# Second phase of a two-phase mixer kernel: the order of the small rounds inside a body changes

## The chip, the cores and the metric

The kernel runs on one core of a Trainium2 chip. The metric is device time in microseconds for one launch. Three runs of the kernel before gave 2612.58, 2613.08 and 2613.16 us; the median is 2613.08 us. One further execution was profiled.

## The reference, cut to what matters

One layer reads a prompt of 4096 tokens and 8 running streams of 16 tokens, all of width 1024. After an RMS norm, one projection feeds two groups of heads: a gated linear attention (4 heads) and an RWKV-7 group (8 heads of 64). The second group is the one that the change touches:

```
xm = p_shift + rwkv_mu * (prev - p_shift)          # token shift
r, kr, vr, wd, ad = jnp.split(xm, ...)             # 512, 512, 512, 64, 64 columns
w = jnp.exp(-DECAY * jax.nn.sigmoid(w0 + jnp.tanh(wd) @ w_up))   # low rank, width 64
a = jax.nn.sigmoid(a0 + ad @ a_up)                 # low rank, width 64
kk = kr * k_k;  kr = kr * (1 + (a - 1) * k_a)
kk = kk / max(sqrt(sum over head of kk*kk), 1e-12) # a sum over each head of 64
S_t = S_{t-1} (diag(w_t) - kk_t^T (a_t*kk_t)) + v_t^T k_t ;  y_t = S_t r_t
y = group_norm(y) * ln_w + ln_b + bonus;  o = y * silu(z_r)
```

Both groups' outputs go through one output projection, a second RMS norm and the residual.

## The kernel before

The program has two phases that follow each other. The first (to about 1004 us) is the gated linear attention group, and is not touched. The second is the RWKV group, cut into 17 blocks of tokens: block 0 holds the 8 streams (128 tokens), blocks 1 to 16 hold 256 tokens of the prompt each. A block is worked off in chunks of 64 tokens, four in a block (two in block 0). The chunks are a chain: the state S after one chunk is needed by the next.

TensorE's work (PE below) falls in two sorts. The filler is the projection of a block from `r_hT`, in six rounds of 48 matmuls (named x4, x6 for the keys, x0, x2 for r, x8, x10 for v, each 2 of 13 column groups) and one of 24 (x12, the low-rank inputs wd and ad); the hi and lo halves of the numbers make three products. A round is issued in thirds of 8 matmuls, called pieces (`piece`, L1616). Small rounds hang on it: `lwa0` and `lwa2` (L1643, the low-rank products for w and a), `kn0` and `kn2` (L1671, the head sums of the squared keys), `xs0` and `xs1` (L1660, the blocks of the triangular matrix), `bs0` and `bs2` (L1671, the head sums for the bonus), `centre` and `variance` (L1817 and L1822, the group norm).

The chain of a chunk is: `meet` (L1765 and L1749, reads S), `scores` of the next chunk (L1695), `unknowns` (L1779), `turn` of the next chunk (L1706, L1709), `solve` (L1719, L1726), `advance` (L1790, new state, and L1803, y), `join` (L1736). `join` waits for `keep_w`, a copy on VectorE (DVE below) of PE's L1726 result from bank B to `r_Wt` (L2208). `next` on DVE (L2243, L2245) makes the new S, for which the next `meet` waits.

The order of all of it is written out by hand in four tables, one an engine: `PE_BODY`, `ACT_BODY`, `DVE_BODY`, `POOL_BODY`, and one for the DMA queue of SyncE (SP), which stays. A table is the order in one body; body e works the chain of block e's four chunks, projects block e + 2, and, for the names with a minus, finishes block e + 1 (`xs`, `bs`, and on GpSimd, POOL below, `kappa`, `r` and `invert`). Numbers behind a colon are the chunk in the body. `out` marks a point at which the jobs of the output projection may be put; in the last two bodies the pieces that have no block left are replaced by pieces of that projection (`room`), which begins at the token x2 of the last body but one. Each engine takes its list strictly in order, and waits on semaphores. There are four PSUM banks for rounds; a round waits until the one four before it has been read.

ScalarE (ACT) does the table functions: `tanh_w` (L1888), `tanh` (L1901, which makes the inputs of `decay`), `squares` (L1911), `gamma` (L1931 to L1937), `rnorm` (L1919, L1921), `deviation` (L1983, L1985), and copies out of PSUM (`taken`, `odd`, `turned`, `z1`, `keep_y`, `join_e`). DVE does `decay` (L2106 and four scans L2109), `clamp` (L2117), `k_factor` (L2133), `unit` (L2126), `k_prime` (L2140, L2141), `even` (L2235, without which `advance` can't start), `beta` (L2157), `a` (L2162), `rkk` (L2149), `mixed` (L2093), `normed` (L2265, four L2268), `gated` (L2275, L2278), `low` (L2282) and `masked` (L2195). POOL inverts the triangular blocks in 60 dependent steps (L1557, L1559), between a store and a load through scratch DRAM on each side; `turn_inverse` on DVE (L2203) then transposes the result, and `solve` of the next block's first chunk, in the last quarter of the body, waits for it.

Of the kernel before, what the change touches and what calls it, by code (L numbers as in the profile page):

```python
# [59 lines left out]
def tiles(b):  # L60

    return 1 if b == 0 else BLK // P
# [58 lines left out]
def nchunks(b):  # L121
    return 2 if b == 0 else 4


def first_chunk(b):
    return CHUNKS.index((b, 0))


def last_chunk(b):
    return first_chunk(b) + nchunks(b) - 1  # L130
# [126 lines left out]
def gla_phase(nc, t, c):  # L257
# [719 lines left out]


PE_BODY = """
    meet:0 scores:1 x12*3 -xs0 -xs1 unknowns:0 turn:1 x4 out x4*3 solve:1 advance:0 join:1 x4*2 -bs0 -bs2 meet:1  # L980
    out scores:2 centre:0 x6*3 unknowns:1 turn:2 x6*2 out x6 variance:0 lwa0 solve:2 advance:1 join:2 x0*4 out
    meet:2 scores:3 x0*2 lwa2 x2 unknowns:2 turn:3 x2*2 out x2*2 solve:3 advance:2 join:3 x2 kn0 kn2 x8 meet:3
    out scores:4 x8*5 unknowns:3 turn:4 centre:1 x10 out x10*2 solve:4 advance:3 join:4 x10*3 variance:1 out
""".split()
ACT_BODY = """
    -deviation:1 taken:x12 -high:1 odd:0 tanh_w out turned:1 z1:1 keep_y:0 join_e:1 taken:x4 out centred:0
    squares:0 odd:1 turned:2 out taken:x6 deviation:0 z1:2 keep_y:1 join_e:2 tanh:lw0 tanh:la0 out squares:2
    high:0 taken:x0 tanh:lw2 tanh:la2 odd:2 turned:3 out gamma keep_y:2 z1:3 join_e:3 taken:x2 rnorm:0 out
    rnorm:2 taken:x8 odd:3 turned:4 centred:1 out z1:4 keep_y:3 join_e:4 taken:x10 load_h out
""".split()  # L990
DVE_BODY = """
    -mixed:x10 -normed:1 masked:1 zc:0 -gated:1 mixed:x12 even:0 -strict:0 out -strict:1 -low:1 keep_w:1 next:0
    join_o:1 -bonus:0 mixed:x4 out zc:1 -bonus:2 masked:2 even:1 out mixed:x6 keep_w:2 normed:0 next:1 join_o:2
    gated:0 out zc:2 low:0 masked:3 mixed:x0 decay out even:2 keep_w:3 next:2 join_o:3 clamp:0 mixed:x2 clamp:2
    out zc:3 k_factor masked:4 unit:0 unit:2 k_prime even:3 mixed:x8 out beta a keep_w:4 next:3 join_o:4 rkk out
""".split()
POOL_BODY = "-kappa -r -invert".split()
SP_BODY = """
# [166 lines left out]
def rwkv_phase(nc, t, c):  # L1165
# [13 lines left out]
    with ExitStack() as ctx:  # L1179
        def sb(name, shape, dt=F32):  # L1180
            return ctx.enter_context(nc.sbuf_tensor("r_" + name, shape, dt))
# [6 lines left out]
        def sig(name, n, size, step=1):  # L1188
            s = Count(ctx.enter_context(nc.semaphore("r_" + name)), name, n, size, step)
            signals.append(s)  # L1190
            return s
# [3 lines left out]
        centre = sb("centre", [P, P])  # L1195
# [77 lines left out]
        def par_s(name, g):  # L1273
            return sc[:, SC[name] + g:SC[name] + g + 1]
# [4 lines left out]
        def plane(b, p):  # L1279
            return ops[:, b % 3, p, :, 0:tiles(b) * P]  # L1280
# [25 lines left out]
        ss_out = sig("ss_out", 8, 1, 16)  # L1306
# [41 lines left out]
        y_full = sig("y_full", 1, NQ)  # L1348
# [504 lines left out]
        def _(act):  # L1853
# [8 lines left out]
            def pair_of(b, r):  # L1862
                n = tiles(b) * P
                act.wait_ge(d_full.sem, d_full.at(ROUND_NO[b, r], 1))
                return bank_of((b, r))[:, 0:2 * n].rearrange("p (g t) -> p g t", g=2)
# [24 lines left out]
            def tanh(arg):  # L1890
                b, r = arg
                n = tiles(b) * P
                pair = pair_of(b, r)
                g0 = int(r[2])
                if r == "lw0" and b:
                    act.wait_ge(op_ok.sem, op_ok.at(b - 1, 2))
                    act.wait_ge(kap_ok.sem, kap_ok.at(b - 1, 2))
                s, bias = (lw_ok, "w0h") if r[1] == "w" else (la_ok, "a0h")
                out = gin[:, :, 0:n] if r[1] == "w" else plane(b, T_)
                for g in range(2):  # L1900
                    act.activation(out[:, g0 + g, :], pair[:, g, :], ACT.Tanh, scale=0.5,  # L1901
                                   bias=par_s(bias, g0 + g)).then_inc(*s.up(b))
# [106 lines left out]
            def out_rstd(tile):  # L2009
# [6 lines left out]
                act.activation(s[:, 3:4], s[:, 2:3], ACT.Exp, scale=-0.5, bias=const(K_LNM)).then_inc(*os_ok.up(tile))  # L2016

            does = {"taken": taken, "tanh_w": tanh_w, "tanh": tanh, "squares": squares, "rnorm": rnorm,
                    "gamma": gamma, "load_h": lambda b: load_h(b + 2), "centred": centred, "deviation": deviation,
                    "high": high_part, "ow_high": split_out, "o_squares": out_squares, "o_rstd": out_rstd,  # L2020
# [376 lines left out]
```

## Time and profile before

| what | value |
|---|---|
| median of three runs | 2613.08 us |
| profiled execution, its own time | 2613.44 us |
| its span | 2611.7 us |
| PE busy | 2480.8 us, 95% |
| ACT, DVE, POOL busy | 51%, 50%, 24% |
| PE clock granted, mean | 0.975 of full |

The span is the time from the first to the last instruction; what lies around it is 1.74 us. Busy is the union of an engine's instructions. PE's matmuls overlap in the array, so that one has a duration of some 270 ns where the next one starts after 109 ns; PE's stalls are read from starts and from the view of waits, not from its busy share. A body has 70.1 us in the middle of the phase.

### The profile page before, as it was taken

The numbers are of one execution on the slowest core, as the hardware profiler recorded it, in microseconds if no ns is written. First come the engines' busy times: TensorE is split into PE (matmuls) and PEld (weight loads), VectorE is DVE, ScalarE is ACT, GpSimd is POOL, SyncE is SP. The second block draws the span as 40 slices with busy tenths as digits, with TensorE's granted clock in tenths as the row PEclk, the third lists the DMA queues.
The fourth block names the chain that finished last, engine by engine and source line by source line (L and its number), as shares of the span: only waits on it lengthen the run. The fifth ranks groups of instructions, "written<-read, shape, count | busy, mean of one in ns | idle before, by whom it ended". The sixth has DMA issues, their size and how long they took to land.

```text
span 2611.7 us, 70434 instructions
## 1 busy us (share of the span) xinstructions
PE 2480.8 (95%) x30628; PEld 1891.0 (72%) x30628; DVE 1295.8 (50%) x2646; ACT 1330.2 (51%) x2368; POOL 623.7 (24%) x1104
## 2 busy tenths in 40 slices
PE   4899999999999995979999999999999997899998
PEld 4677777777777775768888888888888885544443
DVE  4333344433333324456667666776776765442222
ACT  6345566556555544335555555555555553343332
POOL 0000000000000001245555555555555554100000
PEclk9799999999999997989999999999999997999999
DMA  4112222122111112102122212222122214245444
GB/s 188 57 56 76 75 71 66 62 74 89 60 58 53 41 41 76 47 16 72 59 67 67 67 55 67 67 67 59 49 64 56 61 51 146 82 143 159 152 145 137
DMA packets 171027, 202.47 MB, mean 78 GB/s; under 512 B 90080, under 2 KB 125216, under 8 KB 166368
## 3 DMA queue, kind: packets, MB, share of 16 engines
q1 hardware_dynamic: 166352, 180.66, 22.2%
q10 hardware_dynamic: 4368, 17.30, 1.9%
q8 instruction: 243, 3.98, 0.6%
q14 instruction: 64, 0.52, 0.1%
HBM read 117.65 MB, written 80.28 MB: 76 GB/s over the span
## 4 chain that ended last, share of the span: by engine, by line
PE 47%; DVE 4%; POOL 4%; ACT 2%; DMA 2%; issue 1%; SPq 1%; DVEq 0%; POOLq 0%
PE r_d L1616 30%; POOL r_inv L1559 2%; POOL r_inv_tmp L1557 2%; PE r_d L1671 2%; PE r_RZ L1790 2%; PE r_A L1695 1%; PE r_RZ L1765 1%; PE r_A L1719 1%; PE r_d L1643 1%; PE r_d L1660 1%; PE r_RZ L1779 1%; PE r_RY L1803 1%; PE r_d L1817 1%; PE r_RY L1749 1%; PE r_B L1736 1%
## 5 line engine op out<-in xcount | busy, mean ns | idle before, releaser
L1616 PE MATMUL r_d<-r_hT,w_hi 128*128 128x256 f16 (+1 forms) x3536 | 583.4, 272 | 15.2 <-DMA r_hT<-scratch_hT 15.2
L567 PE MATMUL d<-hT,w_hi 128*128 128x256 f16 (+1 forms) x3264 | 525.9, 270 | 1.4 <-DVE hT L840 1.4
L1616 PE MATMUL r_d<-r_hT,w_lo 128*128 128x256 f16 (+1 forms) x1768 | 475.6, 272 | 0.0
L567 PE MATMUL d<-hT,w_lo 128*128 128x256 f16 (+1 forms) x1632 | 436.6, 270 | 0.0
L1616 PEld LDWEIGHTS r_d<-r_hT,w_hi 128*128 128x128 f16 x3536 | 336.7, 99 | 82.4 <-issue 24.3
L567 PEld LDWEIGHTS d<-hT,w_hi 128*128 128x128 f16 x3264 | 315.6, 98 | 51.1 <-issue 12.5
L1557 POOL TENSOR_TENSOR r_inv_tmp<-r_inv 64x30 f32<-64x30 f32 (+14 forms) x480 | 251.6, 524 | 290.5 <-DMA r_inv<-scratch_blocks 254.1
L1616 PE MATMUL r_d<-w_hi,r_ops 128*128 128x512 f16 x1056 | 317.4, 381 | 2.1 <-DVE w_lo L2286 1.7
L1559 POOL TENSOR_TENSOR r_inv<-r_inv,r_inv_tmp 64x30 f32<-64x30 f32 (+14 forms) x480 | 268.9, 560 | 37.6
L1506 POOL MEMSET r_run_s<- 128x128 f16 x1 | 0.2, 205 | 1000.9 <-POOLq L266 1000.9
L1882 ACT ACTIVATE r_praw<-r_d,r_sc 128x256 f32<-128x256 f32 (+1 forms) x221 | 92.5, 467 | 240.9 <-PE r_d L1616 240.8
L1616 PE MATMUL r_d<-w_lo,r_ops 128*128 128x512 f16 x528 | 201.0, 381 | 0.0
L1616 PEld LDWEIGHTS r_d<-w_hi,r_ops 128*128 128x128 f16 x1056 | 103.1, 98 | 129.1 <-issue 7.7
L1616 PEld LDWEIGHTS r_d<-r_hT,w_lo 128*128 128x128 f16 x1768 | 174.3, 99 | 25.6 <-issue 5.2
L567 PEld LDWEIGHTS d<-hT,w_lo 128*128 128x128 f16 x1632 | 160.4, 98 | 17.4
L567 PE MATMUL d<-w_hi,hT 128*128 128x512 f16 x528 | 157.0, 379 | 0.0
L2093 DVE SCALAR_TENSOR_TENSOR r_ops<-r_d,r_sc,r_praw 128x256 f32<-128x256 f32 (+1 forms) x204 | 87.8, 472 | 109.4 <-ACT r_praw L1882 106.9
L2006 ACT ACTIVATE r_xb<-r_d 128x512 f32<-128x512 f32 x66 | 39.5, 598 | 194.1 <-PE r_d L1616 194.1
L2297 DVE TENSOR_TENSOR r_ops<-r_d,w_hi 128x512 f32<-128x512 f32 x66 | 45.6, 691 | 183.0 <-ACT r_xb L2006 182.9
L558 PE MATMUL tr<-diag,x_tok 128*128 128x128 f32 x528 | 74.0, 285 | 36.5 <-DVE diag L832 36.5
L1567 POOL TENSOR_TENSOR r_ops<-r_ops,r_gin 128x1024 f32<-128x1024 f32 (+1 forms) x17 | 38.9, 2290 | 264.5 <-DVE r_scr L2149 264.5
L567 PE MATMUL d<-w_lo,hT 128*128 128x512 f16 x264 | 100.1, 379 | 0.0
(270 smaller groups left out, 4737.6 us busy)
## 6 DMA issues: line engine op xcount, KB each, us to landing
x_tok<-in_x SPq DMA_DIRECT2D x33, 512.0 KB, 4.3
r_ops<-in_x SPq DMA_DIRECT2D x33, 512.0 KB, 4.2
out_y<-r_ops SPq DMA_DIRECT2D x33, 512.0 KB, 2.9
scratch_hT<-hT SPq DMA_DIRECT2D x16, 1024.0 KB, 6.8
r_hT<-scratch_hT ACTq DMA_DIRECT2D x16, 1024.0 KB, 4.8
scratch_mg<-m_hl SPq DMA_DIRECT2D x33, 256.0 KB, 2.0
r_zr<-scratch_zr SPq DMA_DIRECT2D x33, 256.0 KB, 3.3
r_bon<-scratch_bonus SPq DMA_DIRECT2D x33, 256.0 KB, 3.9
```

The costliest lines, as they stand in the source:

```text
L558: mm = pe.matmul(tr_bank[half][:, k * P:(k + 1) * P], x_tok[:, tile % 2, (4 * half + k) * P:(4 * half + k + 1) * P], diag[:, tile % 2, :], ...
L567: mm = pe.matmul(out, lhs(k, a, w), rhs(k, a, w), start=(n == 0), stop=(n == len(terms) - 1))
L1557: step(pool.tensor_tensor(tmp, inv[0:n, 0:u, u:u + 1].to_broadcast([n, u, w]), inv[0:n, u:u + 1, u + 1:32].to_broadcast([n, u, w]), ALU.mult))
L1559: step(pool.tensor_tensor(inv[0:n, 0:u, u + 1:32], inv[0:n, 0:u, u + 1:32], tmp, ALU.add))
L1567: pool.tensor_tensor(plane(b, K_), plane(b, K_), gin[:, :, 0:n], ALU.mult).then_inc(*kap_ok.up(b))
L1616: mm = pe.matmul(out, lhs(k, a, w), rhs(k, a, w), start=(m == 0), stop=(m == 3 * KT - 1))
L1671: mm = pe.matmul(out[:, g * n:(g + 1) * n], headsum[:, :], scr[:, g0 + g, 0:n], start=True, stop=True)
L1790: mm = pe.matmul(half(RZ, 0)[hrows(h), g, :], bu[:, s, h, 0, g, :], uv(h, g), start=True, stop=True)
L1882: ins = act.activation(out[:, g], src[:, g], ACT.Identity, scale=par_s("mu", g0 + g))
L2006: act.activation(o_junk[h], bank_of(("out", tile, h))[:, :], ACT.Square, accum_out=st[:, tile % 2, h:h + 1]).then_inc(*os_ok.up(tile))
L2093: dve.scalar_tensor_tensor(out=out[:, g], in0=pair[:, g], scalar=par_s("mu1", g0 + g), in1=before[:, g], op0=ALU.mult, op1=ALU.add).then_i ...
L2297: dve.tensor_tensor(t_c[:, h * 512:(h + 1) * 512], bank_of(("out", tile, h))[:, :], npost[:, h * 512:(h + 1) * 512], ALU.mult).then_inc(*o ...
```

## The change

The tables are written in another order. On PE, `lwa0` moves from the second chunk of a body to the end of the first, `lwa2` from the third to the second, `kn0` and `kn2` from the end of the third to the end of the second, ahead of most of x0, so that x0, x2, x8, x10 (r and v) come after all that hangs on the keys. `xs1` goes behind `unknowns:0` and `turn:1`, `bs2` behind the next `scores`, `centre:0` and `variance:0` each half a chunk to a chunk later. ACT and DVE follow: `decay`, the clamps, `k_factor`, `unit`, `k_prime`, `beta`, `a`, `rkk`, and `normed:0`, `gated:0`, `low:0` change places. The opening (blocks 0 and 1 before the first chunk) is made from the same tables and changes too. In `tanh` one wait is new: `la0` writes into a plane that an older block's chunks still read. Of the tables the diff shows PE's and DVE's second and third lines.

```diff
 PE_BODY = """
...
-    out scores:2 centre:0 x6*3 unknowns:1 turn:2 x6*2 out x6 variance:0 lwa0 solve:2 advance:1 join:2 x0*4 out
-    meet:2 scores:3 x0*2 lwa2 x2 unknowns:2 turn:3 x2*2 out x2*2 solve:3 advance:2 join:3 x2 kn0 kn2 x8 meet:3
+    meet:1 scores:2 -bs2 x6*3 unknowns:1 turn:2 x6*2 out x6 lwa2 solve:2 advance:1 join:2 centre:0 kn0 kn2 x0*2
+    out meet:2 scores:3 x0*4 unknowns:2 turn:3 variance:0 x2 out x2*2 solve:3 advance:2 join:3 x2*3 x8 meet:3
...
 DVE_BODY = """
...
-    gated:0 out zc:2 low:0 masked:3 mixed:x0 decay out even:2 keep_w:3 next:2 join_o:3 clamp:0 mixed:x2 clamp:2
+    clamp:0 out clamp:2 k_factor masked:3 zc:2 unit:0 unit:2 k_prime out even:2 beta normed:0 keep_w:3 gated:0
...
                 if r == "lw0" and b:
                     act.wait_ge(op_ok.sem, op_ok.at(b - 1, 2))
                     act.wait_ge(kap_ok.sem, kap_ok.at(b - 1, 2))
+                if r == "la0" and b >= 3:
+                    act.wait_ge(y_full.sem, y_full.at(last_chunk(b - 3), 1))
+                    if b == 3:
+                        act.wait_ge(ss_out.sem, ss_out.at(0, 8))
```

Lines of ACT's and DVE's code lie 5 further down in the changed kernel (L2208 is L2213), those of PE's one (L1736 is L1737). Below, DVE in the third chunk of a body. Before, these rows stand between the reading of x0 and the copy for `join:3`:

```order
L2106 TENSOR_SCALAR r_gin<-r_gin 128x1024
L2109 SCALAR_TENSOR_TENSOR r_gin<-r_run_p,r_gin 128x256 x4
L2235 COPY r_bu<-r_RZ 64x256
L2208 COPY r_Wt<-r_B 128x128
L2243 TENSOR_TENSOR r_S<-r_RZ,r_S 128x256
L2245 TENSOR_TENSOR r_S<-r_S,r_gL 128x256
L2213 COPY r_TT<-r_B 32x4x32
```

In the changed kernel, from `unit` to `next:2` in the same chunk:

```order
L2131 SCALAR_TENSOR_TENSOR r_ops<-r_ops,r_sc 128x256 x4
L2145 TENSOR_TENSOR r_ops<-r_ops,r_scr 128x1024
L2146 SCALAR_TENSOR_TENSOR r_ops<-r_ops 128x1024
L2240 COPY r_bu<-r_RZ 64x256
L2162 SCALAR_TENSOR_TENSOR r_ops<-r_ops,r_gin 128x1024
L2270 TENSOR_TENSOR r_yT<-r_yT,r_d 128x512
L2273 TENSOR_SCALAR r_yT<-r_yT,r_sc,r_lnb_s 128x128 x4
L2213 COPY r_Wt<-r_B 128x128
L2280 TENSOR_TENSOR r_yT<-r_yT,r_bon 128x512
L2283 TENSOR_TENSOR r_yT<-r_yT,r_zr 128x512
L2248 TENSOR_TENSOR r_S<-r_RZ,r_S 128x256
```

The copy to `r_Wt` stood right behind the copy to `r_bu` (`even:2`); now `beta` and `normed:0`, six instructions, stand between them, and `unit` and `k_prime`, another six, ahead of `even:2`.

DVE at the end of the second chunk, between the copy for `join:2` and the new state. Before (`normed:0` between them):

```order
L2208 COPY r_Wt<-r_B 128x128
L2265 TENSOR_TENSOR r_yT<-r_yT,r_d 128x512
L2268 TENSOR_SCALAR r_yT<-r_yT,r_sc,r_lnb_s 128x128 x4
L2243 TENSOR_TENSOR r_S<-r_RZ,r_S 128x256
L2245 TENSOR_TENSOR r_S<-r_S,r_gL 128x256
```

In the changed kernel `decay` stands there:

```order
L2213 COPY r_Wt<-r_B 128x128
L2111 TENSOR_SCALAR r_gin<-r_gin 128x1024
L2114 SCALAR_TENSOR_TENSOR r_gin<-r_run_p,r_gin 128x256 x4
L2248 TENSOR_TENSOR r_S<-r_RZ,r_S 128x256
L2250 TENSOR_TENSOR r_S<-r_S,r_gL 128x256
```

The new state of the second chunk now comes behind the scans instead of behind the group norm's scaling.

PE at the end of the second chunk of a body. Before, from `variance:0` to `join:2`:

```order
L1822 MATMUL r_d<-r_y_sq,r_headmean 128x512
L1643 MATMUL r_d<-r_lor,r_up 128x256 x4
L1719 MATMUL r_A<-r_bu,r_sxq 64x64 x8
L1726 MATMUL r_B<-r_TD,r_sxq 32x32 x8
L1790 MATMUL r_RZ<-r_bu 64x64 x8
L1803 MATMUL r_RY<-r_sxq,r_bu 64x64 x8
L1736 MATMUL r_B<-r_TT,r_Wt 32x32 x8
```

In the changed kernel, from `lwa2` to `kn2`:

```order
L1644 MATMUL r_d<-r_lor,r_up 128x256 x4
L1720 MATMUL r_A<-r_bu,r_sxq 64x64 x8
L1727 MATMUL r_B<-r_TD,r_sxq 32x32 x8
L1791 MATMUL r_RZ<-r_bu 64x64 x8
L1804 MATMUL r_RY<-r_sxq,r_bu 64x64 x8
L1737 MATMUL r_B<-r_TT,r_Wt 32x32 x8
L1818 MATMUL r_d<-r_yT,r_centre 128x512
L1672 MATMUL r_d<-r_scr,r_headsum 128x256 x4
```

The low-rank products here were the first pair and are now the second, and the head sums of the keys follow the chain directly.

## Rows read from the trace of the kernel before

**Rows 1.** Stretches: length; busy PE, PEld, DVE, ACT, POOL; PE clock; DMA share; GB/s

```profile
1004.00:1180.00 176.00, 142.12 (x1966) 123.58 (x1968) 84.15 (x212) 63.72 (x126) 61.61 (x134) 0.86 0.20 54
1180.00:2162.00 982.00, 980.09 (x17466) 819.99 (x17461) 681.40 (x1434) 559.77 (x1033) 520.21 (x882) 1.00 0.21 61
...
1460.31:1530.41 70.10, 70.07 (x1251) 58.59 (x1252) 48.94 (x103) 40.21 (x75) 37.38 (x64) 1.00 0.22 62
```

**Rows 2.** PE's waits from 1180 to 2162 us (total, times, longest)

```profile
PE r_B L1726 <- DVE r_TD L2203: 1.5, 3, 0.8
```

**Rows 3.** The chain of waits in that body (start us, us, what)

```profile
1460.31 0.61 PE r_RZ L1765 x16
...
1462.27 2.73 PE r_d L1616 x24
1464.99 2.01 PE r_d L1660 x64
...
1468.34 3.60 PE r_d L1616 x32
1471.94 0.61 PE r_A L1719 x16
...
1474.01 0.37 PE r_B L1736 x16
...
1476.23 1.73 PE r_d L1671 x8
...
1487.80 0.86 PE r_d L1822 x2
1488.65 1.06 PE r_d L1643 x8
```

**Rows 4.** The same body, ACT in order of time (start us, us, instruction)

```profile
1506.24 1.06 ACT L1931 ACTIVATE r_gam<-r_gin 128x1024 f32<-128x1024 f32 x1 [0.72 <-DVE r_gin L2109]
...
1511.00 1.28 ACT L1916 ACT_TABLE_LOAD   x1
...
1515.65 0.72 ACT L1921 ACTIVATE r_ops<-r_ops,consts 128x512 f32<-128x512 f32 x1
```

**Rows 5.** The same body, DVE in order of time

```profile
1463.68 1.12 DVE L2268 TENSOR_SCALAR r_yT<-r_yT,r_sc,r_lnb_s 128x128 f32<-128x128 f32 x4
...
1492.02 2.32 DVE L2268 TENSOR_SCALAR r_yT<-r_yT,r_sc,r_lnb_s 128x128 f32<-128x128 f32 x4
...
1502.38 3.83 DVE L2109 TENSOR_TENSOR_SCAN r_gin<-r_run_p,r_gin 128x256 f32<-128x256 f16 x4
...
1518.24 1.23 DVE L2140 TENSOR_TENSOR r_ops<-r_ops,r_scr 128x1024 f32<-128x1024 f32 x1
...
1520.52 0.41 DVE L2235 COPY r_bu<-r_RZ 64x256 f32<-64x256 f32 x1
...
1521.90 1.22 DVE L2157 SCALAR_TENSOR_TENSOR r_ops<-r_ops,r_gin 128x1024 f32<-128x1024 f32 x1
...
1524.17 0.70 DVE L2203 STREAM_TRANSPOSE r_TD<-r_TT 128x512 f32<-128x512 f32 x1
```

**Rows 6.** The same body, POOL's last step of the inversion

```profile
1516.28 0.35 POOL L1561 TENSOR_SCALAR r_inv<-r_inv 64x32 f32<-64x32 f32 x1
```

**Rows 7.** Two stalls of PE, and the stretch behind each (columns of rows 1)

```profile
2233.00:2237.00 4.00, 0.79 (x33) 0.61 (x27) 0.71 (x1) 0.39 (x1) 0.00 (x0) 1.00 0.43 68
2237.00:2241.00 4.00, 4.00 (x58) 2.90 (x54) 1.59 (x5) 1.79 (x3) 0.00 (x0) 0.57 0.01 4
...
2166.00:2169.00 3.00, 0.76 (x22) 0.62 (x20) 3.00 (x8) 0.00 (x0) 0.00 (x0) 0.96 0.55 218
2169.00:2179.00 10.00, 7.02 (x142) 6.38 (x139) 6.74 (x12) 5.14 (x9) 0.00 (x0) 0.50 0.21 40
```

**Rows 8.** PE's waits, whole program (total, times, longest)

```profile
PE r_A L1706 <- DVE r_sxq L2195: 4.3, 2, 3.6
PE r_d L1660 <- DVE r_ops L2162: 4.3, 1, 4.3
```

More of the change, by code:

```diff
@@ L979 @@
 PE_BODY = """
-    meet:0 scores:1 x12*3 -xs0 -xs1 unknowns:0 turn:1 x4 out x4*3 solve:1 advance:0 join:1 x4*2 -bs0 -bs2 meet:1
-    out scores:2 centre:0 x6*3 unknowns:1 turn:2 x6*2 out x6 variance:0 lwa0 solve:2 advance:1 join:2 x0*4 out
-    meet:2 scores:3 x0*2 lwa2 x2 unknowns:2 turn:3 x2*2 out x2*2 solve:3 advance:2 join:3 x2 kn0 kn2 x8 meet:3
-    out scores:4 x8*5 unknowns:3 turn:4 centre:1 x10 out x10*2 solve:4 advance:3 join:4 x10*3 variance:1 out
+    meet:0 scores:1 x12*3 -xs0 unknowns:0 turn:1 -xs1 x4 out x4*3 solve:1 advance:0 join:1 x4*2 lwa0 -bs0 out
@@ L984 @@
+    meet:1 scores:2 -bs2 x6*3 unknowns:1 turn:2 x6*2 out x6 lwa2 solve:2 advance:1 join:2 centre:0 kn0 kn2 x0*2
+    out meet:2 scores:3 x0*4 unknowns:2 turn:3 variance:0 x2 out x2*2 solve:3 advance:2 join:3 x2*3 x8 meet:3
+    out scores:4 x8*5 unknowns:3 turn:4 centre:1 out x10*3 solve:4 advance:3 join:4 x10*3 variance:1 out
 """.split()
 ACT_BODY = """
-    -deviation:1 taken:x12 -high:1 odd:0 tanh_w out turned:1 z1:1 keep_y:0 join_e:1 taken:x4 out centred:0
-    squares:0 odd:1 turned:2 out taken:x6 deviation:0 z1:2 keep_y:1 join_e:2 tanh:lw0 tanh:la0 out squares:2
@@ L988 @@
-    high:0 taken:x0 tanh:lw2 tanh:la2 odd:2 turned:3 out gamma keep_y:2 z1:3 join_e:3 taken:x2 rnorm:0 out
-    rnorm:2 taken:x8 odd:3 turned:4 centred:1 out z1:4 keep_y:3 join_e:4 taken:x10 load_h out
+    -deviation:1 taken:x12 odd:0 tanh_w turned:1 out -high:1 z1:1 keep_y:0 join_e:1 taken:x4 tanh:lw0 out
+    tanh:la0 odd:1 turned:2 squares:0 out taken:x6 tanh:lw2 tanh:la2 z1:2 keep_y:1 squares:2 join_e:2 centred:0
+    gamma out rnorm:0 rnorm:2 taken:x0 odd:2 turned:3 out deviation:0 z1:3 join_e:3 high:0 keep_y:2 taken:x2 out
@@ L990 @@
+    taken:x8 odd:3 turned:4 out centred:1 z1:4 keep_y:3 join_e:4 taken:x10 load_h out
 """.split()
 DVE_BODY = """
-    -mixed:x10 -normed:1 masked:1 zc:0 -gated:1 mixed:x12 even:0 -strict:0 out -strict:1 -low:1 keep_w:1 next:0
-    join_o:1 -bonus:0 mixed:x4 out zc:1 -bonus:2 masked:2 even:1 out mixed:x6 keep_w:2 normed:0 next:1 join_o:2
-    gated:0 out zc:2 low:0 masked:3 mixed:x0 decay out even:2 keep_w:3 next:2 join_o:3 clamp:0 mixed:x2 clamp:2
-    out zc:3 k_factor masked:4 unit:0 unit:2 k_prime even:3 mixed:x8 out beta a keep_w:4 next:3 join_o:4 rkk out
+    -mixed:x10 zc:0 masked:1 -normed:1 mixed:x12 even:0 -gated:1 -strict:0 out -strict:1 -low:1 keep_w:1 next:0
@@ L996 @@
+    join_o:1 mixed:x4 out -bonus:0 zc:1 masked:2 -bonus:2 even:1 out mixed:x6 keep_w:2 decay next:1 join_o:2
+    clamp:0 out clamp:2 k_factor masked:3 zc:2 unit:0 unit:2 k_prime out even:2 beta normed:0 keep_w:3 gated:0
+    next:2 low:0 join_o:3 mixed:x0 out mixed:x2 masked:4 zc:3 a rkk even:3 mixed:x8 out keep_w:4 next:3 join_o:4
+    out
 """.split()
```

## The prediction, made before the changed kernel ran

> **What bounds the kernel now.** I read the table of busy time by stretches first. The changed phase has three parts [rows 1]: an opening of 176 us in which PE is busy 142 us at 0.86 of its clock, a middle of 982 us with PE busy 980 us at full clock, and an end with stalls. The reader is to see that the middle has nothing to give: the view of PE's waits has 1.5 us in those 982 us, all of them on the transposed inverse [rows 2], and the body of 70.10 us is a train of PE work. The change neither adds nor removes PE work, so the middle can only lose, or stay; gains can come from the opening and the end alone. Next I read one body of the middle in the chain of waits, for PE's durations, and in order of time for ACT and DVE. All places below are counted from the body's first `meet`, +0 being 1460.31 us [rows 3].
>
> **PE's new timetable.** Pieces from [rows 3]: `meet` with `scores` 1.96 (1460.31 to 1462.27), three projection pieces 2.73, both `xs` 2.01, `unknowns` with `turn` about 1.4 (1467.00 to 1468.34), four pieces 3.60, `solve` to `join` 2.07 and `join` itself 0.37, two `kn` or `bs` 1.73, `variance` or `centre` 0.9, a low-rank pair 1.06. In the changed order these add up, without a stall, to 17.8 for the second chunk's `meet`, 35.5 for the third's, and in the third chunk: scores done +37.5, four pieces of x0 +41.1, `unknowns` and `turn` +42.5, `variance` +43.4, three pieces of x2 +46.1, `advance` about +47.1, `join:3` +48.2. The body's sum is as before.
>
> **Who must be there at +48.2.** `join:3` waits for the copy to `r_Wt`, and DVE takes its list in order. I follow the chain back to its start. The second chunk's L1726 is done at +29.6; DVE copies it (done +29.95) and then runs `decay`: 0.7 for the addition and 3.83 for the scans [rows 5], done +34.4. ACT's `gamma` waits for that. Before, it goes from 1506.24 [rows 4], and its two activations of 1.06 and the small copy are 2.3: done +36.9. Then two `rnorm`, 5.37 together (1511.00 to 1516.37, [rows 4], table loads in it): done +42.3. DVE has the clamps, `k_factor` and the masks done by +40 and waits for that. From +42.3: the second `unit` 0.9, `k_prime` 2.28 (1518.24 to 1520.52, [rows 5]), `even:2` 0.34, `beta` 1.14 (1521.90, next instruction behind it), one multiplication of `normed` 0.7, four scalings, copy 0.3. `even:2` comes at +45.9, in time for `advance` at +47.1. The four scalings take 1.12 where POOL is idle (1463.68) and 2.32 in the inversion (1492.02) [rows 5]; the inversion ends at +56.3 [rows 6], so here they are slow. Sum: 42.3 + 0.9 + 2.3 + 0.3 + 1.2 + 0.7 + 2.3 + 0.3 = +50.3 at the least; `join:3` has been waiting since +48.2. Before, the copy for this `join` stood right behind `even:2`, and `join` never waited.
>
> I take 3.0 us a body for this stall. The lower end is 2.1 (sum above). Upper end: `k_prime` and `beta` run in the inversion now, which no row of before shows; if they are slowed as the scalings are in absolute terms, 0.3 us an instruction (2.32 less 1.12, over four), three of them give 0.9; I allow as much again for what differs between bodies, which makes 4.0. 3.0 is the lower end with the 0.9 that the rows bear out.
>
> The Trainium skill bears on this ("SBUF — State Buffer", section "SBUF: two separate sides"): a DVE instruction in a two-port mode or with two SBUF inputs and a GpSimd instruction exclude each other for a whole instruction. The slow scalings agree [rows 5]. By that rule `k_prime` and `beta` wait too, the sum is at the upper end and not the lower, and the inversion loses what they take.
>
> **The clock.** A stall of that length on PE is followed by half clock in the places where the trace has one. Behind the stall in which PE is busy 0.79 of 4 us, the next 4 us have 0.57 with PE busy all through; behind the one with 0.76 of 3 us, 10 us have 0.50 [rows 7]. Full speed is 2.4 GHz, the half 1.2. Where PE is busy with projections, 4 us at 0.57 cost 0.43 x 4 = 1.7 us. Behind `join:3` stand four pieces of projection, dense work, so I take the short kind, and 1.5 us a body. Bounds: 0 (the clock stays), and 5 (10 us at 0.50, all filled).
>
> The Trainium skill ("TensorE: Matmul & The Clock Gate", "What's actually happening") says that the throttled state is the default and activity releases it. By that a drop in every body would be no surprise, and dense work behind it ends it soon.
>
> **What else moves, and costs nothing in a body.** The inversion: `xs1` is 1.4 us later on PE, but DVE's `strict:0` and `strict:1` stood behind `even:0` anyway, which comes 1 us earlier since `unknowns` goes ahead of `xs1`; with `gated:1` ahead of them they end at about +9.3, before at +9.5. SP's queue keeps its order. If POOL's 60 steps get longer by 1 to 3 us, `turn_inverse` has that room, since `solve:4` is itself 3 to 5 us later by the stall, and DVE is freed: before, it reached that point at +63.9 (1524.17) [rows 5] straight from `a`. The one new wait, `la0` for y of an older block, stands behind `keep_y:0`, which has waited for the same; behind it on ACT `odd:1` is queued, 5 us away. `decay` between `join:2`'s copy and the second chunk's new state: S is ready at 34.4 + 0.9 = +35.3 against `meet` at +35.5; hidden by 0.2, and if the cover fails the price is about 0.5 a body. `kn2` wants `squares:2`, at +32.0 against +32.8. Tanh's table load is saved once a body, on an engine that has room.
>
> **Opening and end.** In the opening `kn0` and `kn2` come before x0, so ACT's and DVE's chain for block 0 starts two rounds earlier, and the wait of 4.3 us of `xs0` for `a` [rows 8] shrinks to about 1; each block pays 1.5 us of PE waiting for `squares:2`. The first `turn`'s wait of 3.6 for the mask [rows 8] falls to about 1.5, with the half clock behind it. The third chunk of block 0 has `beta` ahead of its state steps. Together I take -3, bounds -8 and +2. In the last body but one `strict:1` stands behind jobs of the output weights that wait for ACT; ACT's `turned:1` now goes ahead of its half of them, and the last inversion starts some 2 us earlier. `normed:0` ahead of the copy costs about 2 in the same body. I take 0, bounds -4 and +4.
>
> **The sum.** The bodies of blocks 1 to 14 have all of it, a block two ahead whose `k_prime` stands in the third chunk and a tile to normalise: 14 bodies. 14 x (3.0 + 1.5) = 63; opening -3; end 0; the 1.5 us of [rows 2] go: +58.5. Against the profiled execution's own 2613.44 that is 2672; the median of the runs, 2613.08, lies 0.36 below it. I forecast 2671 us.
>
> **Rivals.** (1) The stall, but the clock stays full. For: the trace has only a few stalls to go by, all where the work around them is thinner than in the middle. Against: the one in 3 us of [rows 7] is no longer than the new one, and was followed by it. 14 x 3.0 - 4.5 = +37.5: 2650. (2) Faster, because the wait at `join:3` isn't there. It decides at one point: whether DVE is through with the scalings before +48.2, which it would be if `rnorm` ended 2.1 us earlier than I have it. For: all of it hangs on sums of a dozen durations, and the opening then gives its 3 to 5. Against: `gamma`, the two `rnorm` and the DVE work behind them have no slack to lose, and each has its row. 2613 - 5: 2608. (3) No stall at `join:3`, but POOL is slowed by `unit`, `k_prime` and `beta` inside the inversion by more than the 1.5 us that the inverse has, for which PE has waited three times already [rows 2]: 14 x 1 - 4 = +10: 2623. (4) The stall with the long kind of half clock each time: 14 x (3.0 + 4.5) - 4.5 = +100: 2714.
>
> **How the numbers follow.** Forecast 0.52, (1) 0.24, (2) 0.12, (3) 0.05, (4) 0.07. The range should leave 2 in 10: (2) and half of (4) and (3) are out. The forecast's own ends are 14 x 2.1 + 14 x 0.8 - 8 = +33 and 14 x (4.0 + 2) + 4 = +88; with (1), and its lower end 14 x 2.1 - 6 = +23, the range is 2632 to 2706. A difference of 0.2%, 5 us, is about what can be told from none: faster by more 0.09, within it 0.05, slower by more 0.86.
>
> **What would show it.** In the changed profile, PE's waits from 1180 us on have a line L1737 <- DVE r_Wt L2213 with 14 or 15 times and 30 to 55 us, where before there is 1.5 us in all; in the same body DVE goes without a gap from the second L2131 through L2145, L2146, L2240, L2162, L2270 and L2273 to L2213; each body is 73 to 76 us long; PE's clock in the middle stretch falls below 1.00, to about 0.95; the wait on the inverse is gone there. In the opening the wait L1661 <- L2167 is 1 us in place of 4.3. Wrong would be: a body of 70.1 us, or a stall at another wait (`meet` for S, L1672 for the squares), or a stall of 3 us with the clock at 1.00.

## The result, and the profile after

The changed kernel takes 2684.8 us (median of four runs, 2680.1 to 2687.3) where the kernel before takes 2612.8: ratio 1.0274, 95% interval 1.0256 to 1.0292. It is 72 us slower. The forecast was 2671, the range 2632 to 2706.

The table of busy time by stretches of the changed kernel comes first: the opening and the middle of [rows 1], and one body, which now has 75.05 us (columns as in [rows 1]).

```profile
1004.00:1180.00 176.00, 143.40 (x1970) 122.73 (x1972) 91.76 (x213) 63.55 (x127) 67.37 (x134) 0.87 0.20 55
1180.00:2162.00 982.00, 939.32 (x16279) 776.31 (x16276) 695.99 (x1335) 500.43 (x949) 521.82 (x819) 0.97 0.20 57
1330.99:1406.04 75.05, 71.93 (x1250) 59.52 (x1249) 53.69 (x103) 38.55 (x74) 40.02 (x63) 0.98 0.21 58
```

The opening has hardly changed. In the middle PE is busy for 939 of 982 us instead of 980, and its clock is 0.97 instead of 1.00. A body has the same instructions as before, and DVE is busy in it for 53.7 us instead of 48.9: the same work on DVE has become longer. PE's waits in the middle (total, times, longest), against [rows 2]:

```profile
PE r_B L1737 <- DVE r_Wt L2213: 39.5, 13, 3.2
PE r_RZ L1766 <- DVE r_S L2250: 1.1, 4, 0.4
```

One line has taken the place of the wait for the inverse: `join:3` waits for the copy to `r_Wt`, 3.0 us each time. In the 14 bodies of blocks 1 to 14 (1179.5 to 2235.2 us) it is 42.5 us in 14 times, over the whole program 50.1 us in 18 times; the wait of `xs0` in [rows 8] has gone from 4.3 to 1.0, and a wait of the head sums for the squares is new:

```profile
PE r_B L1737 <- DVE r_Wt L2213: 50.1, 18, 5.1
...
PE r_d L1672 <- ACT r_scr L1916: 4.2, 3, 1.5
...
PE r_d L1661 <- DVE r_ops L2167: 1.0, 1, 1.0
```

The stall and what follows it, by stretches (columns as before):

```profile
1376.50:1379.50 3.00, 2.93 (x72) 2.46 (x71) 3.00 (x4) 2.04 (x4) 2.84 (x3) 1.00 0.00 0
1379.50:1383.00 3.50, 0.45 (x22) 0.31 (x18) 3.46 (x8) 0.00 (x0) 3.09 (x6) 1.00 0.02 5
1383.00:1387.00 4.00, 4.00 (x38) 3.02 (x31) 3.83 (x8) 1.28 (x3) 3.47 (x7) 0.62 0.25 65
```

PE is busy 0.45 of 3.5 us, DVE all through; then PE has four microseconds of dense products at 0.62 of its clock. The granted clock costs 1.7 us in twelve of the 14 bodies and 3.4 in the other two (the first and the thirteenth, of 76.1 and 76.9 us), 27.3 us together. The chain of waits has the same place from PE's side: the four projection pieces behind `join:3` take 5.27 us, where four had 3.60 in [rows 3].

```profile
1383.24 5.27 PE r_d L1617 x32
```

And DVE in order of time, from the copy for `join:2` to the copy for `join:3` (start us, us, instruction, and in brackets the idle time ahead of it):

```profile
1360.87 0.29 DVE L2213 COPY r_Wt<-r_B 128x128 f32<-128x128 f32 x1 [0.16 <-PE r_B L1727]
...
1361.79 3.96 DVE L2114 TENSOR_TENSOR_SCAN r_gin<-r_run_p,r_gin 128x256 f32<-128x256 f16 x4
...
1368.08 2.65 DVE L2138 TENSOR_SCALAR r_scr<-r_ops,r_sc 128x256 f32<-128x256 f32 x4
...
1372.18 2.99 DVE L2131 SCALAR_TENSOR_TENSOR r_ops<-r_ops,r_sc 128x256 f32<-128x256 f32 x4
1375.28 1.40 DVE L2145 TENSOR_TENSOR r_ops<-r_ops,r_scr 128x1024 f32<-128x1024 f32 x1
1376.60 1.61 DVE L2146 SCALAR_TENSOR_TENSOR r_ops<-r_ops 128x1024 f32<-128x1024 f32 x1
...
1380.32 2.22 DVE L2273 TENSOR_SCALAR r_yT<-r_yT,r_sc,r_lnb_s 128x128 f32<-128x128 f32 x4
1382.46 0.28 DVE L2213 COPY r_Wt<-r_B 128x128 f32<-128x128 f32 x1
```

No instruction from the second on, those left out included, has idle time in brackets: the list lasts from 1360.87 to 1382.46, 21.6 us. PE needs 18.7 us from the end of `solve:2` to the point at which it wants `join:3`. That was not in the prediction, which counted from ACT's `rnorm`. In the trace the last step of `rnorm` ends at 1373.44, and DVE, behind its own list, comes to the half of `unit` that reads it at 1373.60, so the two chains meet there within 0.2 us; the experiments take them apart.

```profile
1372.72 0.72 ACT L1926 ACTIVATE r_ops<-r_ops,consts 128x512 f32<-128x512 f32 x1
```

### The profile page after: what moved, and what is told of

It reads as the page before. It is cut to its first block, busy times and chain, and to the rows that moved or that the text cites. A ratio compares the mean times of both kernels' runs of the same rounds, so it can differ in the third digit from the quotient of the medians.

```text
span 2685.6 us, 70433 instructions
## 1 busy us (share of the span) xinstructions
PE 2508.6 (93%) x30628; PEld 1900.6 (71%) x30628; DVE 1368.2 (51%) x2646; ACT 1305.9 (49%) x2354; POOL 667.4 (25%) x1104
## 4 chain that ended last, share of the span: by engine, by line
PE 44%; DVE 13%; issue 2%; POOL 1%; DMA 1%; ACT 1%; SPq 0%; DVEq 0%; POOLq 0%; ACTq 0%
PE r_d L1617 30%; DVE r_gin L2114 2%; DVE r_ops L2131 2%; PE r_A L1696 1%; PE r_d L1672 1%; DVE r_scr L2138 1%; PE r_d L1644 1%; PE r_RZ L1766 1%; PE r_d L1661 1%; DVE r_yT L2273 1%; PE r_RZ L1791 1%; PE r_A L1720 1%; DVE r_ops L2146 1%; PE r_RZ L1780 1%; DVE r_sxq L2200 1%
## 5 line engine op out<-in xcount | busy, mean ns | idle before, releaser
L1617 PE MATMUL r_d<-r_hT,w_hi 128*128 128x256 f16 (+1 forms) x3536 | 607.4, 279 | 14.9 <-DMA r_hT<-scratch_hT 14.3
L1617 PE MATMUL r_d<-r_hT,w_lo 128*128 128x256 f16 (+1 forms) x1768 | 487.7, 278 | 0.0
L1617 PEld LDWEIGHTS r_d<-r_hT,w_hi 128*128 128x128 f16 x3536 | 346.8, 101 | 89.5 <-issue 21.3
L1558 POOL TENSOR_TENSOR r_inv_tmp<-r_inv 64x30 f32<-64x30 f32 (+14 forms) x480 | 277.9, 579 | 447.0 <-DMA r_inv<-scratch_blocks 410.6
L567 PEld LDWEIGHTS d<-hT,w_hi 128*128 128x128 f16 x3264 | 315.6, 98 | 51.4 <-issue 12.6
L1560 POOL TENSOR_TENSOR r_inv<-r_inv,r_inv_tmp 64x30 f32<-64x30 f32 (+14 forms) x480 | 285.3, 594 | 37.6
L1617 PEld LDWEIGHTS r_d<-w_lo,r_ops 128*128 128x128 f16 x528 | 52.0, 99 | 63.2 <-issue 2.1
```

The costliest lines, as they stand in the source:

```text
L567: mm = pe.matmul(out, lhs(k, a, w), rhs(k, a, w), start=(n == 0), stop=(n == len(terms) - 1))
L1558: step(pool.tensor_tensor(tmp, inv[0:n, 0:u, u:u + 1].to_broadcast([n, u, w]), inv[0:n, u:u + 1, u + 1:32].to_broadcast([n, u, w]), ALU.mult))
L1560: step(pool.tensor_tensor(inv[0:n, 0:u, u + 1:32], inv[0:n, 0:u, u + 1:32], tmp, ALU.add))
L1617: mm = pe.matmul(out, lhs(k, a, w), rhs(k, a, w), start=(m == 0), stop=(m == 3 * KT - 1))
```

## The experiments

The kernel before ran beside each group of kernels; its medians there were 2612.7, 2614.1, 2612.2 and 2612.3 us, and ratios are against those.

**The keys behind the join.**

```diff
-    ... zc:2 unit:0 unit:2 k_prime out even:2 beta normed:0 keep_w:3 gated:0
-    next:2 low:0 join_o:3 mixed:x0 out ...
+    ... zc:2 unit:0 out even:2 normed:0 keep_w:3 gated:0
+    next:2 low:0 join_o:3 unit:2 k_prime beta mixed:x0 out ...
```

> The changed kernel with the third chunk's list on DVE in another order: the second unit, k_prime and beta stand behind join_o:3, so that only even:2 and normed stand ahead of the copy for join:3. My theory is that the whole loss is DVE's queue ahead of that copy: by my timetable normed, which waits for the variance at +43.4 and ACT's two steps behind it, is then done at about +48.2 and the copy at +48.5, against join:3 at +48.7, so the stall of 3.1 us and the half clock behind it both go, the body is 70.1 to 70.6 us again, and the time is 2684.8 - 14 x 5 = about 2615 (2608 to 2625). Rival A, the half clock comes from the new order on PE (thinner work round the head sums) and not from the stall: only 14 x 3.1 goes, 2641. Rival B, POOL's inversion, slowed by k_prime and beta beside it, becomes late and PE waits for the transposed inverse instead: 1 us a body or more, 2630.

Measured: 2701.3 us, ratio 1.034 (1.0324 to 1.0355). The time lies outside every branch: it is slower than the changed kernel. Of the mechanisms, rival B's did come, and larger than its number: PE waits for the inverse. PE's waits from 1180 to 2200 us:

```profile
PE r_B L1727 <- DVE r_TD L2208: 26.2, 13, 2.1
PE r_B L1737 <- DVE r_Wt L2213: 21.9, 13, 1.9
PE r_RZ L1780 <- DVE r_Zc L2226: 13.4, 9, 1.7
```

The wait at `join:3` fell from 3.0 to 1.7 us and two others came up. For the first, DVE and ACT in order of time show the reason:

```profile
1379.63 0.69 DVE L2270 TENSOR_TENSOR r_yT<-r_yT,r_d 128x512 f32<-128x512 f32 x1 [4.27 <-ACT r_d L1990]
```
```profile
1372.10 1.28 ACT L1921 ACT_TABLE_LOAD   x1
...
1377.03 1.28 ACT L1986 ACT_TABLE_LOAD   x1
...
1379.02 0.58 ACT L1990 ACTIVATE r_d<-r_d 128x512 f32<-128x512 f32 x1
```

DVE stands idle for 4.27 us because `normed` now waits for ACT's `deviation`, which is behind the table loads of `rnorm` and has one itself. ACT's queue lay right below DVE's. The wait for the inverse has DVE's moved work ahead of its transpose, and POOL beside that: the two one-row copies around the last read of x8 took 2.20 and 1.31 us beside POOL's `kappa` and `r`, where such copies take 0.16.

```profile
1397.74 2.20 DVE L2094 COPY r_praw<-r_carry 128x2 f32<-128x2 f32 x1
...
1400.77 1.31 DVE L2103 COPY r_carry<-r_praw 128x2 f32<-128x2 f32 x1
```
```profile
1397.57 2.35 POOL L1568 TENSOR_TENSOR r_ops<-r_ops,r_gin 128x1024 f32<-128x1024 f32 x1 [5.96 <-DVE r_scr L2154]
```

**Group norm behind the copy.**

```diff
-    ... even:2 beta normed:0 keep_w:3 gated:0
+    ... even:2 beta keep_w:3 normed:0 gated:0
```

> The changed kernel with one exchange on DVE: normed:0 stands behind the copy for join:3 instead of ahead of it. My theory is that DVE has too much to do between rnorm and the fourth chunk's meet, and not only a bad place for one copy: join:3 then waits 0.3 us (beta ends 0.3 us behind the time at which it is wanted), but the new state of next:2, behind normed and gated, is ready at about +55.1 where meet:3 wants it at about +53.0: 2 to 3.5 us of wait at meet:3 in every body, half clock behind it as before, and a time within 10 us of the changed kernel's, 2675 to 2690. The rival, that the place of the copy alone does it, says 2612 to 2620 and no new wait.

Measured: 2682.1 us, ratio 1.0265 (1.025 to 1.028), a time as expected. The new wait at `meet:3` is there too, but not on S, as expected, but on y, which ACT copies behind `high`, and `high` waits for `gated`:

```profile
PE r_RZ L1766 <- ACT r_yT L1955: 34.8, 13, 2.8
PE r_B L1737 <- DVE r_Wt L2213: 2.8, 13, 0.3
```

So the copy's place is only where the queue shows. Taking it out of the queue moves a wait of 2.7 us by one step of PE.

**PE kept at work in the stall.**

```diff
-    ... solve:3 advance:2 join:3 x2*3 x8 meet:3
+    ... solve:3 advance:2 fill join:3 x2*3 x8 meet:3
+            def fill(arg):       # the first 8 products of x2's second half
...
+                for _ in range(3):
```

> The changed kernel with three pieces of x2 (24 products, 2.7 us at full clock) computed once more than needed in the gap ahead of join:3 of the bodies, their sums thrown away, so that PE is busy while it would wait. If the half clock behind the stall comes from PE standing still, it goes: join:3 is where it was or 0.1 later, the four pieces behind it take 3.6 us and not 5.3, the granted clock of the middle is 0.99 to 1.00, and the time falls by 14 x 1.8 = 25 us, to about 2660 (2655 to 2665). If the clock falls for another reason (periodically, or by PE's load of work), the pieces behind are as slow as before and the time stays at 2685 or rises, since the extra products at half clock take 5.4 us and end behind the copy.

Measured: 2662.4 us, ratio 1.0188 (1.0171 to 1.0205): 22.4 us less than the changed kernel. The stretches at the same place (PE's join is at 1380.45) and the wait that is left:

```profile
1377.50:1381.50 4.00, 3.62 (x47) 3.00 (x45) 3.93 (x8) 0.27 (x1) 3.53 (x7) 1.00 0.00 0
1381.50:1385.50 4.00, 4.00 (x66) 3.52 (x67) 3.83 (x11) 1.75 (x4) 3.45 (x8) 1.00 0.45 132
```
```profile
PE r_B L1748 <- DVE r_Wt L2224: 4.1, 12, 0.6
```

From the start of `solve:3` to the join PE needs 5.44 us, in the changed kernel 5.33, so the copy comes no earlier; the clock stays at 1.00. With nothing else changed this shows that PE's standing still brings the half clock, and what it costs: in the traces the 14 bodies are 23.6 us shorter than the changed kernel's, 1.7 each. The medians differ by a little less; the filling also runs once ahead of block 1, without such a stall, and block 1 starts 1.7 us later.

**Shorter ACT ahead of `unit`.**

```diff
             def rnorm(arg):
                 b, g0 = arg[0], int(arg[1])
-                act.preload_act_table_set(LN_SET)
```

> The changed kernel without the two activation table loads in rnorm; gamma ahead of it has loaded the same table, and only copies stand between. ACT's two rnorm then end 2 x 1.28 = 2.56 us earlier, and if the chain rnorm, unit, k_prime, beta, normed, copy is what join:3 waits for, with nothing else beside it, the stall falls from 3.1 to about 0.5 us in every body. With the clock full behind so short a stall the body is 70.8 us and the time 2685 - 14 x 4.4 = 2623 (2618 to 2630); with the half clock still behind it, 2685 - 14 x 2.6 = 2649. The rival, that the chain is bound elsewhere (DVE's own work or the inversion's hold on its inputs), says that the wait hardly moves: 2675 or more.

Measured: 2680.4 us, ratio 1.0258 (1.0242 to 1.0273). Here the rival was right: the wait has not moved.

```profile
PE r_B L1737 <- DVE r_Wt L2212: 39.4, 13, 3.1
```

In the trace the loads are gone and the last step of `rnorm` ends at 1366.79, but DVE begins `unit` at 1368.37 behind its masks and needs 10.5 us to the copy, busy all through:

```profile
1368.37 3.00 DVE L2130 SCALAR_TENSOR_TENSOR r_ops<-r_ops,r_sc 128x256 f32<-128x256 f32 x4
...
1378.65 0.28 DVE L2212 COPY r_Wt<-r_B 128x128 f32<-128x128 f32 x1
```

The chain that I had priced is not the one that ends last. The 4 us that the kernel does gain come from the opening: its joins there are 3.2 to 4.3 us earlier (1085.7 and 1169.6 us, in the changed kernel 1088.9 and 1173.9), and no body is shorter.

**Without the inversion, in both kernels.**

```diff
+                if 2 <= b <= 14:
+                    for _ in range(60):
+                        step(pool.nop())
-                if b == 0:
+                elif b == 0:
```

> The changed kernel with POOL's 60 steps of the inversion left out in blocks 2 to 14 (each step an empty instruction; the blocks' inverses are not computed). The trace of the changed kernel has DVE busy without a gap from the copy for join:2 to the copy for join:3, 21.6 us, where PE needs 18.7, and the instructions in it that ran alone before are 0.35 us slower each beside the inversion. My theory now: it is this list of DVE work, drawn out by the inversion, that join:3 waits for. Without it unit falls from 2.99 to 1.66, k_factor from 2.65 to 1.53, k_prime from 3.0 to 2.45, normed's scalings from 2.22 to 1.12, and the copy comes 2.5 to 4 us earlier, bounded then by ACT's rnorm and deviation: a stall of 0 to 0.7 us, a body of 70 to 71 us, 2612 to 2630. The rival is the chain that I predicted from, ACT's gamma and two rnorm with the DVE steps behind them: the scalings alone gain, 1.1 to 1.9 us, the stall stays at 1.2 to 2 us with the half clock behind it, 2655 to 2670.

> The control: the kernel before with the same 60 steps left out in blocks 2 to 14. PE waits 1.5 us for the inverse in the middle, and nothing else hangs on it: 2611 to 2613. If the inversion cost the kernel before something that its waits don't show, 2605 or less.

Measured: the changed kernel 2626.7 us, ratio 1.0045 (1.0032 to 1.0059); the kernel before 2613.1, ratio 0.9992 (0.9983 to 1.0001). So some 59 of the 72 us hang on the inversion beside the new order (12.6 are left), and none of the time before did. Block 15's inversion, which runs in the last of the 14 bodies, is kept, and that body still has 75.45 us. The same DVE list in a body without it:

```profile
1350.63 0.29 DVE L2216 COPY r_Wt<-r_B 128x128 f32<-128x128 f32 x1 [0.16 <-PE r_B L1730]
...
1351.56 2.43 DVE L2117 TENSOR_TENSOR_SCAN r_gin<-r_run_p,r_gin 128x256 f32<-128x256 f16 x4
...
1356.32 1.37 DVE L2141 TENSOR_SCALAR r_scr<-r_ops,r_sc 128x256 f32<-128x256 f32 x4
...
1360.52 0.88 DVE L2134 SCALAR_TENSOR_TENSOR r_ops<-r_ops,r_sc 128x256 f32<-128x256 f32 x2 [0.30 <-ACT r_ops L1929]
1363.22 0.88 DVE L2134 SCALAR_TENSOR_TENSOR r_ops<-r_ops,r_sc 128x256 f32<-128x256 f32 x2 [1.82 <-ACT r_ops L1929]
...
1369.80 0.28 DVE L2216 COPY r_Wt<-r_B 128x128 f32<-128x128 f32 x1
```

From copy to copy 19.2 us, of which DVE is idle for 3.0 (0.90 ahead of the masks and the two gaps shown): 16.1 us of work, where it was 21.6. Now it is ACT's `rnorm` for which `unit` waits, twice, and the stall that is left is 0.8 us in each of the 13 bodies, and 3.0 in the one that has its inversion:

```profile
PE r_B L1740 <- DVE r_Wt L2216: 13.5, 14, 3.0
```
```profile
1369.00:1372.00 3.00, 2.20 (x42) 1.88 (x39) 2.93 (x9) 0.83 (x2) 0.00 (x0) 1.00 0.02 5
1372.00:1376.00 4.00, 4.00 (x84) 3.48 (x82) 3.23 (x11) 1.30 (x4) 0.00 (x0) 1.00 0.75 233
```

The predicted chain is there after all; it is the one below. Behind a stall of 0.8 us the clock stays full, and the body is 70.96 us. Without the stall that is 70.16; in the control it is 70.00, so PE's new order costs by itself 0.2 us a body at the most, some 2 us in all.

**The keys behind the join, and no reload.** DVE with the edit of the first run, and also `beta` behind `zc:3` and `rkk` behind `join_o:4`; ACT without the loads in `rnorm` and `deviation`.

> The changed kernel with less in each of the three lists that came last in turn. DVE: the second unit and k_prime behind join_o:3, beta behind zc:3, rkk behind join_o:4, so that POOL's kappa and r start behind the last transpose. ACT: no table loads in rnorm and deviation, whose table is there already. In the run with the keys behind, normed waited for deviation (ACT, 4.3 us idle on DVE) and the copy for join:3 came 1.8 us late; rnorm's and deviation's loads are 3.8 us of that queue, of which 1.3 are on the path: stall 0 to 0.5 us. The wait of 2.1 us for the inverse goes with rkk and POOL's hold behind it, that of 1.5 for Zc with beta. If PE then has next to no wait the clock is full: 2610 to 2620. The rival, that the new order leaves DVE more than it can do in a body wherever it stands, says that another wait of 1 us or more a body comes up: 2630 or more.

Measured: 2626.5 us, ratio 1.0052 (1.0038 to 1.0065), body 71.5 us, clock 1.00 in the middle. The wait at `join:3` is gone from the middle; 0.8 us a body for Zc are left. The expected range missed by 7 us, and the rival by 3; the wait for Zc, which I had taken as gone, is some 10 of the 20 us by which the 14 bodies are longer than 14 of 70.0 us.

```profile
PE r_RZ L1780 <- DVE r_Zc L2224: 9.9, 12, 1.0
PE r_B L1727 <- DVE r_TD L2206: 2.1, 5, 0.8
```

**The same with Zc first.** `mixed:x2` also behind `zc:3`.

> The run with the keys behind and no reload, with mixed:x2 also moved behind zc:3. That run's trace has 0.8 us a body of waiting for Zc (L1780, 13 times, 10.6 us) and else 2 to 3 us in the middle. If DVE's list ahead of zc:3 is the cause, that goes: 2626.5 - 10 = 2616 (2613 to 2620), which is parity with the kernel before; PE's new order has no price of its own. If the wait turns up elsewhere, 2623 or more.

Measured: 2619.4 us (2614.3 to 2627.4), ratio 1.0037 (1.0023 to 1.0051). The wait for Zc is gone, as the first branch said, and the time lies in its range; but a wait for the inverse has grown, as the second said, so the agreement in time is in part luck:

```profile
PE r_B L1727 <- DVE r_TD L2206: 8.8, 11, 2.3
```

The new order reaches the old one but for some 7 us, and doesn't pass it.

**The opening alone.** The kernel before, with the opening made from the changed tables and the bodies from its own.

```diff
-    for part in [opening_jobs(PE_BODY)] + ...
+    for part in [opening_jobs(PE_OPEN)] + ...
```

> The kernel before with only the opening (blocks 0 and 1 ahead of the first chunk) in the changed order, the bodies as before. The prediction had -3 us for opening and first body together, the changed kernel's trace has the first meet 0.6 us earlier and the third body's start 0.1 us earlier. By the trace: 2611.5 to 2613.5, no difference. By the prediction: 2609 to 2610. If the first body's own losses (three waits for the squares, one for the stall) hide a gain of the opening, it shows here too: 2608 to 2610.

> The kernel before with only the opening in the changed order, once more with more rounds beside the other: 2610 where before has 2613 (ratio 0.9985 to 0.9995), if the first measurement's 3.0 us are real; 1.000 if they were the spread of the runs.

Measured: 2611.1 us, ratio 0.9987 (0.9978 to 0.9996), and again 2609.3, ratio 0.9991 (0.9982 to 1.0000): 3.0 us each time, the second interval just reaching 1. The opening by itself makes the time shorter by what the prediction said. In its trace the joins in and behind the opening are 5.3 to 6.3 us earlier than before (1087.0 for 1093.3, 1187.9 for 1193.3), and 2.3 at the end (2287.5 for 2289.8). So the stretch itself gains about twice as much, and the last bodies lose 4 of it again; why was not looked into. In the changed kernel the first join has 4.4 of it, the next one 0.5 (1142.8 for 1143.3).

**The opening, and no reload.** The same, with the loads out of `rnorm` and `deviation`.

> The version that the runs point to for beating both kernels: bodies as before, the opening in the changed order (3.0 us faster by itself), and no table loads in rnorm and deviation. In the bodies the loads lie on an engine with room: nothing. In the opening, blocks 0 and 1 pass through rnorm with DVE and PE behind it, so up to 2 x 2.6 us of loads are on the path: 3 to 6 us faster than before, 2607 to 2610 where before has 2613. The rival, that the opening's path runs through PE's sample states and the mask and not through rnorm, says 3 us as with the opening alone.

Measured: 2616.5 us, ratio 1.0019 (1.001 to 1.0029): slower than before. A new wait in every body, and ACT in order of time behind it:

```profile
PE r_RZ L1785 <- DVE r_S L2263: 16.0, 14, 1.4
```
```profile
1342.89 1.28 ACT L2001 ACT_TABLE_LOAD   x1
...
1344.86 1.28 ACT L2003 ACT_TABLE_LOAD   x1
```

Where `tanh` stands ahead of `deviation`, as in the bodies before, the line that I took out was the one that named one table for the logarithm and the exponential. Without it the trace has a load ahead of each, 14 times in the middle. By the Trainium skill ("ScalarE: Activation LUTs", "Table sets: the hidden batching unit") a logarithm followed by an exponential needs one load, since one set has both; this trace has two.

**The opening, and no reload in `rnorm`.**

> The opening in the changed order, bodies as before, and the loads taken out of rnorm only. The last version took them out of deviation too, and there its trace shows two loads where the kernel before has one (one ahead of the logarithm, one ahead of the exponential, since tanh's table stands there), and a new wait for S of 16 us in 14 times behind it. Without that the bodies are as before. If rnorm's loads are on the opening's path: 2 to 5 us under the opening alone, 2606 to 2609 where before has 2613. If the path of the opening doesn't run through them: as with the opening alone, 2610.

Measured: 2606.5 us, ratio 0.9981 (0.9972 to 0.9989), 2.8 us under the opening alone beside it: the fastest, and faster than both kernels.

## Why the prediction was right, and where it was not

- **The middle can only lose; PE's timetable.** Right: `join:3` was predicted for +48.2 and is wanted at +48.7. Without the inversion the body is 70.1 and its stall, to 0.1 us. ([rows 2] has one small wait more in its view, 0.2 us for S.)
- **Stall at `join:3`, 3.0 us a body (2.1 to 4.0).** The size is right (3.0 us in every one of the 14 bodies), the chain is not the one that decides. "DVE has the clamps, k_factor and the masks done by +40 and waits for that": in the trace DVE gets there at +41.2 and doesn't wait. `k_factor` and `unit` are in the inversion too and lose 1.3 and 1.2 us there (2.65 for 1.37, 2.99 for 1.76), which the sum left out: it had the slowing on the four scalings and, as an allowance of 0.9, on `k_prime` and `beta`, of which the trace has 0.6. `rnorm` ends at +42.45 (+42.3 said), and there the two chains are 0.2 us apart; from there to the copy they have the same instructions, so that the size came out right although the chain was the other one, which is in part luck. Cutting ACT's chain by 2.6 us changed nothing, lifting the inversion's hold on DVE left 0.8 us; that both together would leave nothing is likely, but no run has both. The sum that decides is 21.6 us of DVE work against 18.7 of PE's.
- **Half clock, 1.5 us a body (0 to 5).** 1.7, by the run that filled the stall; by the granted clock 1.7 in twelve bodies and 3.4 in two, 1.95 on average. The rivals with full clock and with the long half clock fall: it was the short one in twelve bodies of 14, and twice as long in the other two.
- **14 bodies, +63.** Twelve bodies are 75.0 to 75.4 us, two 76.1 and 76.9, and the 14 together are 72.9 us longer than before (1055.8 for 982.9). 42.5 is the stall and 27.3 the clock. Of the 3 that are left, 2 are the 0.16 us a body that PE's order has in the run without the inversion, and the rest is about what S came late (up to 0.4 in four bodies, a price of about 0.5 that I named and left out).
- **Opening, -3.** In the changed kernel nothing of it is left: block 1's first meet is 0.1 us earlier than before. The opening alone does make the time 3.0 us shorter, but its own stretch gains 5 to 6, so that the agreement with the 3 is in part luck. The changed kernel is 4.4 us ahead at the first join of the phase and 0.6 at the first meet, where the changed bodies begin. Between the two it has a low-rank pair and a pair of head sums more, which PE does later in the kernel before; up to the second join (0.5 ahead) waits for the squares (1.5) and for Zc (1.1) keep it from winning that back. The rest was not taken apart. **End, 0.** +1.1.
- **Rival "no stall" (2608)** would have needed DVE earlier by 3 us and not `rnorm` by 2.1, as its run shows. **Rival "POOL slowed":** POOL was busy for 667 us instead of 624, and the wait for the inverse stayed away in the middle (`solve:4` is later by the stall; that this is the reason is argued, not tested); it came with the three runs that moved DVE's work behind the join.
- **The signs.** From 1180 us on the wait came 17 times (14 or 15 said) with 49.7 us (30 to 55 said), DVE had no gap, the clock (0.97, 0.95 said) and 12 of the 14 bodies (73 to 76 us said) agree. The range, 2632 to 2706, is some 5 us wider at each end than the sums given for it (+23 and +88).

Between the profiled executions the change is 73.9 us (2687.34 less 2613.44) where the forecast had 58.5; the median after is 2.6 below the profiled one. Of these 15.4 us, 11.4 are in the bodies (clock 6.3, PE's order 2.2, stall 0.5; the rest is mostly the 1.5 us taken off for the inverse, in whose place S came late), 2.9 in the opening, 1.1 at the end. The term that was mis-sized most is the clock.

## What to carry to other kernels

Before moving work into a stretch, add up what the waiting engine has to do between two of its copies, at the durations that it has in that stretch, and compare that with what the other engine needs between the same two points; a chain counted back from one late input finds only one of several near-ties. A stall of three microseconds in an otherwise dense stretch of PE cost more than half as much again in clock, and filling it with spare products gave that back. An instruction that looks redundant can be what another one rests on: look at what stands ahead of it in each order.

## What of the hardware was not expected

The inversion slowed much of DVE's work and not only what reads two tensors of SBUF: 5.4 us in the list between the two copies, `unit` 2.99 to 1.76 without it, `k_factor`, with one tensor input, 2.65 to 1.37, the scans 3.96 to 2.43, while `L2270`, which reads a bank of PSUM, has 0.68 with it and 0.69 without, and `beta` 1.22 and 1.21. The Trainium skill ("SBUF — State Buffer", "SBUF: two separate sides") has GpSimd and DVE shut each other out for a whole instruction in two-port modes and with two SBUF inputs; the copy of two elements that took 2.20 us beside POOL's 2.35 agrees with that, since the two end together (1399.94 and 1399.92). So do three of POOL's steps beside `k_prime` and `beta`: they take 1.4 us each, and the next ones, of nearly the same size, 0.5.

```profile
1378.68 1.43 POOL L1560 TENSOR_TENSOR r_inv<-r_inv,r_inv_tmp 64x198 f32<-64x198 f32 x1
...
1380.76 0.53 POOL L1560 TENSOR_TENSOR r_inv<-r_inv,r_inv_tmp 64x184 f32<-64x184 f32 x1
```

The length of a stall does not settle alone whether the clock falls behind it. In the middles of all traces together, none of the 54 stalls of PE between 0.7 and 1.65 us was followed by half clock, 15 of the 26 between 1.65 and 2.45 us were, and so were all 37 of 2.65 us and more. In the first run two stalls of 2.1 us for the late inverse look alike, and the clock fell behind the first and not behind the second (length; PE busy; clock, DMA share, GB/s). What tells the two apart, these rows do not show.

```profile
1400.00:1403.00 3.00, 0.93 (x33) 1.00 0.00 0
1403.00:1406.00 3.00, 3.00 (x66) 0.71 0.00 0
...
1478.00:1481.00 3.00, 0.92 (x35) 1.00 0.02 5
1481.00:1484.00 3.00, 3.00 (x63) 1.00 0.00 0
```
